# First mixer: thirteen convolution taps by GpSimd in the attention, and the squares of four query tiles turned by TensorE and summed by ScalarE

## The reference, cut to what matters

```python
proj = h @ w_in
q, k, v, u, mq = jnp.split(proj, SPLITS, axis=-1)
q = rope_partial(rms_norm(q, g_q), positions)        # per head of 64: mean of squares
k = rope_partial(rms_norm(k, g_k), positions)
y_attn = sliding_window_attention(q, k, v, sinks)
# conformer_conv(u): a gate, 31 taps per channel, a layer norm over the 256 channels, silu
a, gate = jnp.split(u, 2, axis=-1)
h = a * sigmoid(gate)
h = conv(h, w_dw, 31 taps, causal) + b_dw
y_conv = silu(layer_norm(h, g_ln, b_ln))
mkv = rms_norm(mem, g_mem) @ w_mem_kv
y_mem = memory_cross_attention(rms_norm(mq, g_mq), rms_norm(mk, g_mk), mv)
x = x + concat([y_attn, y_conv, y_mem]) @ w_out
```

## Time and profile before

| | us |
|---|---|
| median of 3 runs | 2109.09 |
| lowest, highest | 2108.90, 2109.94 |
| the profiled execution | 2109.04 |
| its span | 2106.9 |
| TensorE busy | 2089.5 (99%) |
| VectorE busy | 1248.7 (59%) |
| ScalarE busy | 787.0 (37%) |
| GpSimd busy | 298.8 (14%) |

### The profile page before, as it was taken

How to read it: one execution, slowest core, us unless ns; L and a number is a source line. 1 busy time by engine, 2 the same in 40 slices (tenths; PEclk the granted TensorE clock), 3 DMA queues, 4 the chain that set the end, 5 groups by cost and what they waited for, 6 DMA issues and landing times.

```text
span 2106.9 us, 28195 instructions
## 1 busy us (share of the span) xinstructions
PE 2089.5 (99%) x9944; PEld 1715.2 (81%) x9944; DVE 1248.7 (59%) x1844; ACT 787.0 (37%) x1091; POOL 298.8 (14%) x357
## 2 busy tenths in 40 slices
PE   9999999999999999999999999999999999999999
PEld 8888888887888888877767888888888888888887
DVE  7666544787676654465996676654466456333332
ACT  6222333547442223344366442223343234222222
POOL 0122400650212230024300212210000000000000
PEclk9999999999999999999999999999999999999999
DMA  5565333320345642323310346542333222222232
GB/s 193 181 194 196 93 110 111 118 94 2 110 162 188 200 136 83 96 96 116 101 31 1 104 157 198 184 145 81 96 106 108 93 90 100 100 93 97 76 96 87
DMA packets 79571, 243.31 MB, mean 115 GB/s; under 512 B 12784, under 2 KB 13424, under 8 KB 79376
## 3 DMA queue, kind: packets, MB, share of 16 engines
q1 hardware_dynamic: 61376, 189.61, 27.6%
q0 software_dynamic: 18128, 52.84, 8.0%
HBM read 235.84 MB, written 2.29 MB: 113 GB/s over the span
## 4 chain that ended last, share of the span: by engine, by line
PE 91%; DVE 6%; ACT 1%; issue 1%; DMA 1%; SPq 0%; ACTq 0%; DVEq 0%
PE ps L710 28%; PE ps L712 28%; PE ps L711 28%; PE ps L1009 2%; DVE ps L1979 2%; PE ps L991 1%; PE ps L970 1%; DVE tmp L1623 1%; DVE small L1877 1%; PE ps L1133 0%; DVE ropA L1850 0%; DVE qA L1852 0%; PE ps L741 0%; DMA w_raw<-in_up 0%; PE ps L728 0%
## 5 line engine op out<-in xcount | busy, mean ns | idle before, releaser
L710 PE MATMUL ps<-h_hi,w_hi 128*128 128x512 f32 x1888 | 740.1, 392 | 1.4 <-DVE h_lo L1922 0.9
L712 PE MATMUL ps<-h_hi,w_lo 128*128 128x512 f32 x1888 | 734.9, 389 | 0.0
L711 PE MATMUL ps<-h_lo,w_hi 128*128 128x512 f32 x1888 | 734.8, 389 | 0.0
L1580 DVE TENSOR_TENSOR w_lo<-w_raw,w_hi 128x1024 fp32r<-128x1024 f32 x336 | 411.5, 1226 | 384.7 <-ACT w_hi L1216 370.3
L1216 ACT ACTIVATE w_hi<-w_raw 128x1024 fp32r<-128x1024 f32 x383 | 402.3, 1052 | 242.7 <-PE ps L712 240.6
L710 PEld LDWEIGHTS ps<-h_hi,w_hi 128*128 128x128 f32 x1888 | 353.6, 187 | 82.4 <-issue 7.5
L712 PEld LDWEIGHTS ps<-h_hi,w_lo 128*128 128x128 f32 x1888 | 353.6, 187 | 75.5
L711 PEld LDWEIGHTS ps<-h_lo,w_hi 128*128 128x128 f32 x1888 | 353.7, 187 | 72.8 <-issue 0.2
L710 PE MATMUL ps<-hid_hi,w_hi 128*128 128x512 f32 x704 | 273.9, 389 | 0.0
L711 PE MATMUL ps<-hid_lo,w_hi 128*128 128x512 f32 x704 | 273.9, 389 | 0.0
L712 PE MATMUL ps<-hid_hi,w_lo 128*128 128x512 f32 x704 | 273.9, 389 | 0.0
(11 more groups left out here) (309 smaller groups left out, 1760.1 us busy)
## 6 DMA issues: line engine op xcount, KB each, us to landing
ada_raw<-in_ada_w POOLq DMA_DIRECT2D x96, 512.0 KB, 4.9
w_raw<-in_gate SPq DMA_DIRECT2D x88, 512.0 KB, 3.5
w_raw<-in_up SPq DMA_DIRECT2D x88, 512.0 KB, 3.3
w_raw<-in_down SPq DMA_DIRECT2D x64, 384.0 KB, 3.1
w_raw<-in_down SPq DMA_DIRECT2D x64, 320.0 KB, 2.8
w_raw<-in_w_mix_c SPq DMA_DIRECT2D x24, 512.0 KB, 3.2
w_raw<-in_w_mix_b SPq DMA_DIRECT2D x17, 512.0 KB, 3.4
w_raw<-in_w_mix SPq DMA_DIRECT2D x16, 512.0 KB, 3.2
```

The source lines that it names most:

```text
L710: pe.matmul(dest, s_hi, m_hi, start=first and n == 0, stop=False)
L711: pe.matmul(dest, s_hi, m_lo, start=False, stop=False)
L712: mm = pe.matmul(dest, s_lo, m_hi, start=False, stop=last and n == len(pairs) - 1)
L1580: dve.tensor_tensor(chunk(w_lo, slot, WT), chunk(w_raw, slot, WT), f32(chunk(w_hi, slot, WT)), ALU.subtract).then_inc(w_lo_done, 1)
```

## The change

The last thirteen taps of chunk 1 go to GpSimd. TAPS_AT loses one tap in step 11 and one in step 12, so VectorE does 49, all in the projections, and none in the attention. GpSimd does the remaining 13 in a function `late_taps`, called between the w_lo of job 18 and that of job 19. Each tap is two instructions: a multiplication of the gated input by the column into the second half of hsA, and an addition to conv. Each waits for the one before it. The first waits for VectorE's last tap and for the last reader of that half of hsA. CONV_FROM = 13 takes the place of LATE_TAPS in the steps of the layer norm, which all move two steps back, except that the four variance products stand together in step 22. The total of step 15 waits for GpSimd's last tap.

The squares of qA0 to qA3 are no longer summed by products with two columns. TensorE turns the four 128x128 blocks into bank 7, and ScalarE reads them with eight activations of 64 columns each, whose sum over the row goes into the tile qstd; what they write otherwise goes back over the squares. The next such turning waits for these. The root over the 48 columns becomes one over the 32 in qstd and one over the 16 of mq0 and mq1 in PSUM.

```diff
-        TAPS_AT = {2: 3, 3: 3, 4: 6, 5: 6, 6: 5, 7: 6, 8: 3, 9: 5, 10: 5, 11: 5, 12: 4}
+        TAPS_AT = {2: 3, 3: 3, 4: 6, 5: 6, 6: 5, 7: 6, 8: 3, 9: 5, 10: 5, 11: 4, 12: 3}
+        CONV_FROM = 13
...
+        TURNED_SQUARES = [t for t in SQUARES if t[:2] == "qA"]
+        sq_kept = Marks(sem("sq_kept"), TURNED_SQUARES)
...
+            def late_taps():
+                at = PAD_A + T
+                after(pool, d_conv, (CONV_A - LATE_TAPS - 1, 1))
+                after(pool, sq_read, "mk1")
+                for t in range(CONV_A - LATE_TAPS, CONV_A):
+                    if t > CONV_A - LATE_TAPS:
+                        after(pool, g_conv, t - 1)
+                    pool.tensor_scalar(chunk(hsA, 1), glu[:, at + t:at + t + T], col("w_dw", CONV_A + t), None, ALU.mult)\
+                        .then_inc(g_tap.at(t), 1)
+                    after(pool, g_tap, t)
+                    pool.tensor_tensor(chunk(conv, 1), chunk(conv, 1), chunk(hsA, 1), ALU.add).then_inc(g_conv.at(t), 1)
+
             for j in range(LEAD, len(TILES_A) + KC):
+                if j == len(TILES_A) + LEAD:
+                    late_taps()
                 split(first_job["mixA"] + j)
...
+                if t in TURNED_SQUARES:
...
+                    for b in range(TT):
+                        mm = pe.transpose(bank(4 if t[1] == "B" else 7)[:, b * P:(b + 1) * P],
+                                          squares_of(t)[:, b * P:(b + 1) * P], mats[:, 0:P])
+                    mm.then_inc(sq_read.at(t), 1)
+                    return
...
-                if u == LATE_TAPS + 2:
-                    after(pe, d_conv, (CONV_A - 1, 1))
+                if u == CONV_FROM + 2:
+                    after(pe, g_conv, CONV_A - 1)
...
+            def keep_squares(t):
+
+                after(act, sq_read, t)
+                turned_, first = bank(4 if t[1] == "B" else 7), QUERIES[t[1] == "B"].index(t) * 2 * TT
+                for n in range(2 * TT):
+                    kept = act.activation(squares_of(t)[:, n * HD:(n + 1) * HD], turned_[:, n * HD:(n + 1) * HD], ACT.Identity,
+                                          accum_out=qstd[:, first + n:first + n + 1])
+                kept.then_inc(sq_kept.at(t), 1)
...
                 if m < len(TILES_A):
                     lead(J + m)
+                if t in TURNED_SQUARES:
+                    keep_squares(t)
...
             def conv_part(u):
-                if 1 <= u <= LATE_TAPS:
-                    conv_tap(CONV_A - LATE_TAPS - 1 + u, 1)
```

More of the change, by code:

```diff
@@ L452, in build @@
         TAB = ["ang", "turns", "whole", "r1p", "r1", "r2p", "r2", "r3p", "r3", "clamp"]
-        d_conv = Marks(sem("d_conv"), [(t, c) for c in range(2) for t in range(CONV_A)])
+        d_conv = Marks(sem("d_conv"), [(t, c) for c in range(2) for t in range(CONV_A)][:2 * CONV_A - LATE_TAPS])
+        g_tap = Marks(sem("g_tap"), range(CONV_A - LATE_TAPS, CONV_A))
+        g_conv = Marks(sem("g_conv"), range(CONV_A - LATE_TAPS, CONV_A))
         d_misc = Marks(sem("d_misc"),
@@ L905, in head_sum @@
                 hs = hsA if mats is matsA else hsB
+                if t in TURNED_SQUARES:
+                    if t == "qB0":
+                        after(pe, h_std, "kB1")
+                    elif t == "qA0":
+                        after(pe, a_misc, "mem_std")
+                    else:
+                        after(pe, sq_kept, TURNED_SQUARES[TURNED_SQUARES.index(t) - 1])
+                    for b in range(TT):
[3 more added lines that the diff above has]
+                    return
                 if is_query(t):
@@ L909, in head_sum @@
                         after(pe, h_std, "kB1")
-                    if t == "qA0":
-                        after(pe, a_misc, "mem_std")
+                    if t == "mq0":
+                        after(pe, sq_kept, TURNED_SQUARES[-1])
                     q = QUERIES[t[1] == "B"].index(t)
@@ L1064, in sumsA @@
                     mm.then_inc(p_misc.at("conv_total"), 1)
[L1065 to L1071, removed]
+                if u == CONV_FROM + 9:
+                    after(pe, d_misc, "conv_sqs")
+                    for b in range(TT):
+                        mm = pe.matmul(bank(5)[:, b:b + 1], hsA[:, b * P:(b + 1) * P], ones[:, 0:1], start=True, stop=True)
+                    mm.then_inc(p_misc.at("conv_var"), 1)
                 if u == len(PAIRS_A) + 2:
@@ L1362, in query_std @@
             def query_std(which, count):
+                done = 2 * TT * len(TURNED_SQUARES) if which == "A" else 0
                 after(act, sq_read, QUERIES[which == "B"][-1])
-                act.activation(qstd[:, 0:count], bank(4 if which == "B" else 7)[:, 0:count], ACT.Sqrt, bias=tiny[:, 0:1],
+                if done:
+                    after(act, sq_kept, TURNED_SQUARES[-1])
+                    act.activation(qstd[:, 0:done], qstd[:, 0:done], ACT.Sqrt, bias=tiny[:, 0:1], scale=1.0 / HD)
+                act.activation(qstd[:, done:count], bank(4 if which == "B" else 7)[:, done:count], ACT.Sqrt, bias=tiny[:, 0:1],
                                scale=1.0 / HD).then_inc(a_misc.at("std" + which), 1)
@@ L1479, in conv_part @@
             def conv_part(u):
[L1481 to L1482 removed]
+                if u in (CONV_FROM + 5, CONV_FROM + 6):
+                    for c in [u - CONV_FROM - 5]:
                         after(act, d_misc, f"ctr{c}")
```

13 lines of the change are left out of this document (8 added, 5 removed).

## The result

The changed kernel takes **2117.29 us** (median of 6 runs, 2114.29 to 2119.02) where the kernel before takes 2108.99 (6 runs beside them, 2107.41 to 2109.94): a ratio of 1.0037, interval 1.0027 to 1.0047, 8.3 us slower. Predicted were 2119.7 with a range of 2112.0 to 2124.0. The profiled execution of the changed kernel is its fastest, 2114.29 us with a span of 2112.5, which is 5.25 us above the profiled execution of before.

What follows compares the result with a forecast made beforehand. TensorE, busy nine tenths or more throughout, was taken as the bound, so any new wait is paid in full. 2109.04 - 1.6 (squares and two taps) + 10.0 (GpSimd wait) + 2.3 (clock) = 2119.7 us, range 2112.0 to 2124.0.

Steps and rivals of the forecast that it cites:

- The squares on TensorE: Squares of qA0 to qA3: turning saves TensorE 0.37 us a tile, 1.5 in all; ScalarE's eight sums take 2.8 us.
- The wait for the reciprocal is gone.: First memory key, before the attention: VectorE 1.58 us earlier, TensorE's 0.94 us wait vanishes; both edits together worth 1.6 us.
- A tap on GpSimd: Thirteen taps on GpSimd: 1.88 multiplication, 1.30 addition, 0.17 waits, 3.35 us each, 43.6 in all, done at 508.3.
- +10.0: Step 16's score, behind the convolution's total that waits for GpSimd's last tap, starts at 510.2 instead of 500.18: 10.0 us lost.
- TensorE at its wait at 496.9: Windowed attention: VectorE without eleven taps lets TensorE gain 1.5 us and reach its wait at 496.9, hidden under 11 us waiting.
- The moved steps of the layer norm, put at nothing: Variance products together in step 22 and centring two steps later keep their order, last reader in step 25: cost nothing.
- The clock, +2.3: Behind TensorE's 11 us wait the clock drops to 1.2 GHz for one pair: 2.3 us lost, ends 0 and 4.6.
- The sum: Whole kernel, from the profiled execution before: 2109.04 - 1.6 + 10.0 + 2.3 = 2119.7 us; chance 0.48.
- the cheap column: Rival: the column operand costs GpSimd nothing, tap 2.96 us, done at 503.2; total 2112.3 or 2114.6 us; chance 0.17.
- GpSimd is quick: Rival: multiplication takes 0.62 us, tap 2.09, GpSimd done at 491.9 before TensorE comes; total 2105.9 us; chance 0.07.

Runs made afterwards that it cites:

- experiment 7: Changed kernel without turned squares and with the convolution's total two steps later (step 17), thirteen taps still on GpSimd: 2108.90 us, 1.0000 of the kernel before.
- experiment 5: Changed kernel with its thirteen late GpSimd taps left out, the second chunk's convolution unfinished: 2109.79 us, 0.9992 of the kernel before.
- experiment 6: Changed kernel without turned squares, GpSimd's tap multiplication written as two operations (times the column, plus 0.0): 2111.78 us, 1.0013 of the kernel before.
- experiment 4: Changed kernel with twelve unread 128x128 products on TensorE ahead of its wait for GpSimd's last tap: 2113.95 us, 1.0028 of the kernel before.
- experiment 2: Changed kernel without turned squares, the thirteen GpSimd taps and the total left where the change puts them: 2117.61 us, 1.0037 of the kernel before.
- experiment 1: Changed kernel with only the turned squares, all taps on VectorE and the total as in the kernel before: 2110.25 us, 1.0007 of the kernel before.
- experiment 3: Changed kernel with the convolution's total two steps later, asking for GpSimd's last tap in step 17: 2110.73 us, 1.0016 of the kernel before.
- experiment 8: Turned squares alone, taps on VectorE as before, plus ten unread products ahead of TensorE's wait for the reciprocal: 2109.35 us, 0.9998 of the kernel before.

## Why the prediction was right, and where its steps were not

The forecast of a slower kernel held, and so did its cause: TensorE waits in step 15 for the thirteenth tap, and the clock is lower behind that wait. That the median came within 2.4 us of the forecast is in part luck, since its steps missed in both directions. One by one:

- **The squares on TensorE.** Right in size: from the turns of vA to the squares of mq0 TensorE takes 30.48 us (411.36 to 441.84) instead of 32.21 (411.90 to 444.11); that is 1.73 for four tiles, 0.43 each, forecast 0.37. ScalarE's eight sums take 1.75 us (418.37 to 420.12) and not 2.8: each is two instructions of about 0.2 us that overlap. Both estimates erred on the careful side.
- **"The wait for the reciprocal is gone."** Wrong, and this is the failed step. I let VectorE be ready 1.58 us earlier for its two taps fewer, with bounds of 0.5 and 2.4 for what GpSimd's later work might do to a rotary product. The reciprocal came 0.76 us earlier on the clock, but 0.54 of that stands already at the turns of vA, where nothing is changed yet (the kernels of this study reach them between 410.9 and 411.9). What the edits are worth here is 0.22, outside even the bounds. GpSimd did not follow TensorE's 1.7 us. Its weight halves start at 440.24 (before, behind the same low part of the memory, at 439.93) and run without a pause until 455.6, where in experiment 7, without turned squares, a pause falls beside a rotary product. The timelines of GpSimd, after and experiment 7, and of VectorE, after and experiment 7:

```profile
440.24 15.38 POOL L629 TENSOR_TENSOR w_lo<-w_raw,w_hi 128x512 fp32r<-128x512 f32 x10
```

```profile
450.48 2.99 POOL L629 TENSOR_TENSOR w_lo<-w_raw,w_hi 128x512 fp32r<-128x512 f32 x2 [1.74 <-ACT w_hi L1250]
```

```profile
441.60 1.71 DVE L1899 TENSOR_TENSOR ropA<-qnA,ada_raw 128x512 f32<-128x512 f32 x1
...
449.65 1.44 DVE L1899 TENSOR_TENSOR ropA<-qnA,ada_raw 128x512 f32<-128x512 f32 x1
451.01 1.77 DVE L1901 TENSOR_TENSOR ropA<-pTA,ada_raw 128x512 f32<-128x512 f32 x1
```

```profile
449.28 0.69 DVE L1899 TENSOR_TENSOR ropA<-qnA,ada_raw 128x512 f32<-128x512 f32 x1
449.88 0.69 DVE L1901 TENSOR_TENSOR ropA<-pTA,ada_raw 128x512 f32<-128x512 f32 x1
```

  In experiment 7 the product at 442.24 takes 0.69 us too, so three products take 2.9 us more with turned squares than without. Without them the wait is gone and A is 1.0 us shorter than before; with them, where the clock holds, 0.2. On this path the turned squares cost 0.8 us, and TensorE, which they bring there earlier, idles 2.4. I had named GpSimd's shift, and let its idle time before 462.17 take it up; I asked whether GpSimd had time, not who works beside it in that time. Whether GpSimd is late for ScalarE's sums or for its own queue was not tried.
- **A tap on GpSimd.** 3.02 us instead of 3.35, 39.1 us for all instead of 43.6. The mis-sized term is the multiplication: 1.57 us, near the row with an immediate (1.49) and not the one with a column (1.87), as the last part of the prediction allowed. The addition, forecast 1.30, takes 1.27. With 4.5 us less on GpSimd the "+10.0" becomes +5.5, and 41.29 - 34.79 = 6.5 less 1.0 for the low clock in the total is just that.
- **TensorE at its wait at 496.9.** It came at 503.11 - 3.54 = 499.57, which is 500.3 on the clock of before, 3.4 late. The gain of 1.5 us that I expected from VectorE's eleven taps exists (1.6 us in experiment 5), but only with a silent GpSimd; the held small operations cost about 3. I had seen them as 0.5 us a pair under the wait, and there they did lie as long as GpSimd was later than TensorE. The wait is 3.5 us and not 11 because GpSimd is done 4.5 earlier and TensorE comes 3.4 later than forecast; and the held operations are why removing the wait (experiments 6, 7) gives no gain.
- **The moved steps of the layer norm, put at nothing.** They cost 0.4 us: C is 23.23 or 23.24 in experiments 4, 5 and 6, which have them where the change puts them and a full clock there, and 22.88 before. Which of the moved steps costs it was not tried.
- **The clock, +2.3.** Right in size behind the wait for GpSimd: 1.7 us in the profile of after (1.0 in the total, 0.7 in the stretch behind it), 2.3 in that of experiment 2 (1.9 and 0.4), 2.7 to 3.3 in the medians of experiment 4. The Trainium skill's rule for an idle array (TensorE: Matmul & The Clock Gate, Part 1: The HAM clock gate), on which one term rested, agrees with both traces in which TensorE idled 3.5 us, after and experiment 2. There was no term for a second fall, behind the wait for the reciprocal.
- **The sum.** Against before's 2109.04: -0.8 for all up to the first score, +5.5 for GpSimd, +1.7 for the clock, +0.4 for the moved steps, -1.3 ahead of the second attention and +0.1 elsewhere give a span 5.6 us longer (as measured; the time, which holds 0.4 less around the span, 5.25). The other 3 us of the median are explained in part. Behind the reciprocal the clock falls in the profiles of experiments 1, 3, 4 and 5 but not in that of after, its fastest run, at a mean clock of 0.999 where the other five show 0.996 or 0.997. That it fell there in those five is inferred, no trace of one of them was taken; it would be worth 1.9 us, by experiment 4. The rest can be a longer low clock behind GpSimd's wait, which lasts 3.4 us in after and 6.8 in experiment 2, or one in the second attention as in experiments 2, 5 and 6, which cost 6.4, 4.7 and 1.6 us there. The mean clock of a run doesn't tell where it was low, so this stays open.

Of the rivals, the cheap column (2114.6 with the clock's term, 0.17) was the nearer to the profiled execution and to the truth about the tap; the median lies nearer to the forecast because errors of -4.5 (the tap) and +3 (the median above the profiled execution, for which there was no term) met, which is luck. The rival "GpSimd is quick" is disproved as a gain: its tap of 2.15 us gives 2111.8, where I had worked out 2105.9.

## What to carry to other kernels

Work moved to an engine that stands idle is not free for its neighbour: before moving it, look at what VectorE runs in the same stretch, and count each operation with two SBUF inputs, however small, as held until GpSimd lets go. Where an engine is made faster ahead of a wait, ask what the wait then costs; a wait of TensorE that grows from 1 to 2.5 us can lose more by the clock than the edit saved. And put the reader of a long side job so late that its worst duration still fits: the total two steps later took away 5.9 to 6.6 of the 8.3 us.

## What the runs showed of the hardware that I had not expected

- A GpSimd TENSOR_SCALAR of 128x512 f32 with one operation and a column takes 1.57 us, with a second operation that adds 0.0 only 0.70. Both hold VectorE's operations on two SBUF inputs for the same 0.70 us.
- A VectorE operation on 128x2 elements, 0.16 us alone, lasts up to 1.20 us beside a GpSimd addition.
- The clock's answer to idle time is not the same from run to run. TensorE idled 2.44 us in the profile of after and 2.42 in those of experiments 3 and 4, at the same instruction: in the first the clock stayed, in the others it was at 0.50 for 6.8 us, at a price of 3.0 in A. After 2.9 us and more it fell each time (experiments 1 and 5 at the reciprocal, experiment 2 and after at GpSimd's wait), and in experiment 8 after 1.64 us, behind a filling of 2.4. It falls behind shorter idle times too: near 1155 us, behind 1.18 us for ScalarE's turned exponentials, in experiments 2, 5 and 6, but not in after with the same 1.18. What tells these cases apart I leave open.
